# Hybrid DSA/S5 block: x normalised ahead of the gain, single feature tiles handed to the first product, one shared angle table

## The reference, cut to what matters

```python
h    = rms_norm(x, g_norm)              # x (512, 2048), g_norm (2048,)
proj = h @ w_in                         # q, k, v, att_gate, q_idx, k_idx, w_idx, u, ssm_gate, merge
q, k, q_idx, k_idx = partial_rotary(...)       # cos/sin of positions * inv_freq, on the first quarter of each head
att  = dsa_attention(q, k, v, q_idx, k_idx, w_idx)     # indexer scores, top 128 keys, softmax
y_a  = (att * silu(att_gate)) @ w_att_out
s    = gelu(s5_ssm(u, a_re, a_im, log_dt, b, c, d))    # dt = exp(log_dt), per group of 16 channels
s    = s * sigmoid(s @ w_glu + b_glu)
y_b  = (s * silu(ssm_gate)) @ w_ssm_out
gates = sigmoid(merge + b_merge)
out  = rms_norm(x + (gates[0] * y_a + gates[1] * y_b) @ w_out, g_final)
```

## Time and profile before

| | |
|---|---|
| median of 3 runs | 1247.41 us (1247.03 to 1248.04) |
| the profiled execution's own time | 1248.48 us |
| its span, first to last instruction | 1246.7 us |
| PE busy | 1194.5 us, 96% |
| DVE busy | 742.8 us, 60% |
| ACT busy | 415.7 us, 33% |
| POOL busy | 40.4 us, 3% |
| mean granted clock of TensorE | 0.986 of full |

### The profile page before, as it was taken

How to read it: one execution, slowest core, us unless ns; L and a number is a source line. 1 busy time by engine, 2 the same in 40 slices (tenths; PEclk the granted TensorE clock), 3 DMA queues, 4 the chain that set the end, 5 groups by cost and what they waited for, 6 DMA issues and landing times.

```text
span 1246.7 us, 13230 instructions
## 1 busy us (share of the span) xinstructions
PE 1194.5 (96%) x5356; PEld 965.2 (77%) x5356; DVE 742.8 (60%) x1265; ACT 415.7 (33%) x557; POOL 40.4 (3%) x26
## 2 busy tenths in 40 slices
PE   3989799999999999999999999999999999999996
PEld 3789688888787788887666666788888888887885
DVE  5977448999836543258999999744233333513224
ACT  5422233332345442233324342342322222413113
POOL 2000000000000000000101010000000000000002
PEclk8989899999999999999999999999999999999998
DMA  8235332323322124232322222233333333346223
GB/s 267 68 94 113 66 102 68 102 68 102 101 68 68 35 70 115 86 96 77 85 75 68 68 68 68 68 101 102 101 101 94 85 91 101 101 136 236 85 85 135
DMA packets 178637, 119.12 MB, mean 96 GB/s; under 512 B 21777, under 2 KB 169489, under 8 KB 177297
## 3 DMA queue, kind: packets, MB, share of 16 engines
q1 hardware_dynamic: 165920, 117.41, 32.8%
q10 hardware_dynamic: 12656, 0.88, 0.7%
HBM read 114.08 MB, written 4.19 MB: 95 GB/s over the span
## 4 chain that ended last, share of the span: by engine, by line
PE 83%; DVE 12%; ACT 2%; DMA 1%; ACTq 1%; issue 1%; POOLq 0%; SPq 0%; DVEq 0%
PE bank L395 20%; PE bank L396 20%; PE bank L397 20%; PE bank L628 4%; PE bank L630 4%; PE bank L629 4%; DVE w_lo L930 2%; DVE score L1055 2%; DVE small L1054 2%; PE bank L527 1%; PE bank L508 1%; PE bank L565 1%; PE bank L566 1%; DVE score L1043 1%; PE bank L580 1%
## 5 line engine op out<-in xcount | busy, mean ns | idle before, releaser
L395 PE MATMUL bank<-act_hi,w_hi 128*128 128x512 f32 (+1 forms) x1088 | 426.8, 392 | 7.5 <-DVE w_lo L930 7.5
L396 PE MATMUL bank<-act_lo,w_hi 128*128 128x512 f32 (+1 forms) x1088 | 419.3, 385 | 0.0
L397 PE MATMUL bank<-act_hi,w_lo 128*128 128x512 f32 (+1 forms) x1088 | 419.1, 385 | 0.0
L930 DVE TENSOR_TENSOR w_lo<-w_raw,w_hi 128x2048 fp32r<-128x2048 f32 (+1 forms) x98 | 223.5, 2281 | 195.9 <-ACT w_hi L653 194.9
L395 PEld LDWEIGHTS bank<-act_hi,w_hi 128*128 128x128 f32 x1088 | 205.9, 189 | 62.9 <-issue 19.2
L397 PEld LDWEIGHTS bank<-act_hi,w_lo 128*128 128x128 f32 x1088 | 205.8, 189 | 39.1
L396 PEld LDWEIGHTS bank<-act_lo,w_hi 128*128 128x128 f32 x1088 | 206.1, 189 | 34.3
L653 ACT ACTIVATE w_hi<-w_raw 128x2048 fp32r<-128x2048 f32 (+1 forms) x98 | 186.4, 1902 | 106.6 <-DMA w_raw<-in_w_out 105.7
L820 ACT ACTIVATE e_prod<-e_tab,rot 128x64 f32<-128x64 f32 (+1 forms) x64 | 31.8, 496 | 148.6 <-DVE e_tab L1233 90.8
L628 PE MATMUL bank<-w_hi,act_hi 128*128 128x512 f32 x192 | 74.7, 389 | 0.0
L629 PE MATMUL bank<-w_lo,act_hi 128*128 128x512 f32 x192 | 74.7, 389 | 0.0
(11 more groups left out here) (230 smaller groups left out, 1386.7 us busy)
## 6 DMA issues: line engine op xcount, KB each, us to landing
w_raw<-in_w_in SPq DMA_DIRECT2D x68, 1024.0 KB, 5.6
w_raw<-in_w_out SPq DMA_DIRECT2D x16, 1024.0 KB, 5.5
w_raw<-in_w_att_out SPq DMA_DIRECT2D x8, 1024.0 KB, 5.5
xt<-in_x SPq DMA_DIRECT2D x4, 1024.0 KB, 10.0
w_raw<-in_w_ssm_out SPq DMA_DIRECT2D x4, 1024.0 KB, 5.1
res<-in_x SPq DMA_DIRECT2D x4, 1024.0 KB, 11.5
out_dram<-res SPq DMA_DIRECT2D x4, 672.0 KB, 3.1
out_dram<-res SPq DMA_DIRECT2D x4, 352.0 KB, 3.4
```

Source lines behind the costliest of these rows:

```text
L395: nc.tensor.matmul(out_ap, wh, x_hi[k], start=(j == 0), stop=False)
L396: nc.tensor.matmul(out_ap, wh, x_lo[k], start=False, stop=False)
L397: last = nc.tensor.matmul(out_ap, wl, x_hi[k], start=False, stop=(j == n - 1))
L930: v.tensor_tensor(w_lo[:, u % SLOTS, 0:n_el], w_raw[:, u % SLOTS, 0:n_el], w_hi[:, u % SLOTS, 0:n_el].bitcast(F32), ALU.subtract).then_inc ...
```

## The change

- The gain leaves the token-major form. `g_row`, `xg` and POOL's two multiplications go. DVE multiplies x by 1/rms alone (one `tensor_scalar` per token tile); the gain of a feature tile is a column (`small[:, G_COL + k]`) and is applied when the turned tile leaves its bank: as the scale of ACT's copy and in DVE's `scalar_tensor_tensor`.
- The hand-over is by feature tile. PE turns feature tiles 0 to 5 of each token tile as it comes (six banks, each with the four token tiles side by side), then, inside the kidx product, four squares of tile k+6 and two matmuls of tile k. The 16 matmuls with the low part of the weights stand at the end.
- POOL takes `w_lo` of unit 0 and both `w_hi` and `w_lo` of unit 1 (semaphores `early_high`, `early_split`; `wait_split` on PE). POOL first fills the rotary tables with ones and zeros.
- The angles are computed once: rows 0 to 15 and 64 to 79 hold the indexer's frequencies, rows 32 to 63 the heads'. Six Sin activations on 32 rows each follow. The angles now stand behind all of `act_lo` and before `w_lo` of unit 2, and `w_lo` of unit 3 stands directly behind the rotation of the indexer key.
- The small parameters are loaded as rows at the very start, by seven transfers from ACT's queue ahead of its first activation. PE turns the 104 rows in one transpose; DVE copies the columns out. The nine element-wise transfers (six on ACT, three on SP) go.

```diff
@@ sync
             sp.dma_start(ident[:, :], c_ident).then_inc(ident_loaded, 16)
-            sp.dma_start(g_row[:, :], g_norm.to_broadcast([P, D])).then_inc(g_loaded, 16)
...
-                sp.dma_start(g_cols[:, 0:32], b_merge[0].rearrange("(c p) -> p c", p=P)).then_inc(ssm_loaded, 16)
-                sp.dma_start(g_cols[:, 32:36], b_glu[0].rearrange("(c p) -> p c", p=P)).then_inc(ssm_loaded, 16)
-                sp.dma_start(g_cols[:, 36:40], d_skip[0].rearrange("(q g) c -> (g c) q", q=QUADS)).then_inc(ssm_loaded, 16)
@@ gpsimd
-            pool.wait_ge(g_loaded, 16)
-            for i, t in enumerate((1, 2)):
-                pool.wait_ge(x_loaded[t], 16)
-                pool.tensor_tensor(xg[:, i, :], xt[:, t, :], g_row[:, :], ALU.mult).then_inc(xg_ready, 1)
+            for table in (rot_idx, rot_head):
+                pool.memset(table[:, 0, :], 1.0).then_inc(table_set, 1)
+                pool.memset(table[:, 1, :], 0.0).then_inc(table_set, 1)
+            pool.wait_ge(rows_loaded, 7 * 16)
...
+            pool.wait_ge(h_ready, TOK)
+            pool.wait_ge(high_done, 1)
+            pool.tensor_tensor(w_lo[:, 0, 0:n_el], w_raw[:, 0, 0:n_el], w_hi[:, 0, 0:n_el].bitcast(F32), ALU.subtract
+                               ).then_inc(early_split, 1)
+            pool.wait_ge(raw_loaded[1], 16)
+            pool.wait_ge(early_split, 1)
+            pool.tensor_scalar(w_hi[:, 1, :], w_raw[:, 1, :], 1.0, 1.0, ALU.mult, ALU.mult).then_inc(early_high, 1)
+            pool.wait_ge(early_high, 1)
+            pool.tensor_tensor(w_lo[:, 1, :], w_raw[:, 1, :], w_hi[:, 1, :].bitcast(F32), ALU.subtract).then_inc(early_split, 1)
@@ tensor
+            for t in range(TOK):
+                if t == TOK - 2:
+                    pe.wait_ge(rows_ready, 1)
+                    pe.wait_ge(rows_loaded, 7 * 16)
+                    nc.tensor.transpose(banks[7][:, 0:N_ROWS], row_tile[0:N_ROWS, :], ident[0:N_ROWS, 0:N_ROWS]).then_inc(rows_turned, 1)
+                pe.wait_ge(h_ready, t + 1)
+                for k in range(6):
+                    last = turn_x(t, k)
+                    if t == TOK - 1:
+                        last.then_inc(h_turned, 1)
...
+            for k in range(KD):
+                pe.wait_ge(h_low, k + 1)
+                if k + 6 < KD:
+                    for t in range(TOK):
+                        last = turn_x(t, k + 6)
+                    last.then_inc(h_turned, 1)
+                wh = w_hi[:, 0, k * width:(k + 1) * width]
+                nc.tensor.matmul(kidx_out, wh, h_hi[k], start=(k == 0), stop=False)
+                nc.tensor.matmul(kidx_out, wh, h_lo[k], start=False, stop=False)
+            wait_split(0)
+            for k in range(KD):
+                last = nc.tensor.matmul(kidx_out, w_lo[:, 0, k * width:(k + 1) * width], h_hi[k], start=False, stop=(k == KD - 1))
@@ scalar
+            for at_row, src in ((0, a_re ...), (PAIRS, a_im ...), (48, g_norm ...), (64, b_merge ...), (96, b_glu ...), (100, d_skip ...)):
+                act.dma_start(row_tile[at_row:at_row + src.shape[0], :], src).then_inc(rows_loaded, 16)
+            act.dma_start(small[32:32 + PAIRS, LDT_COL:LDT_COL + 2], log_dt[0].rearrange("(j g) -> j g", g=2)).then_inc(rows_loaded, 16)
...
+            for t in range(TOK):
+                rms_of(t)
+            high_through(0)
+            act.wait_ge(cols_ready, 1)
+            for k in range(KD):
+                act.wait_ge(h_turned, k + 1)
+                nc.scalar.activation(act_hi[:, k, :], banks[1 + k % 6][:, :], ACT.Copy, scale=small[:, G_COL + k:G_COL + k + 1]
+                                     ).then_inc(h_high, 1)
+            high_through(2)
...
+            act.wait_ge(ang_ready, 1)
+            for table, first, to, n_ in ((rot_idx, 0, 0, 32), (rot_idx, IDX_DIM, IDX_DIM, 32), (rot_head, 32, 0, 32)):
+                here, there = slice(first, first + n_), slice(to, to + n_)
+                nc.scalar.activation(table[there, 1, :], ang[here, 0, :], ACT.Sin, scale=cols[here, 1:2]).then_inc(table_done, 1)
+                nc.scalar.activation(table[there, 0, :], ang[here, 1, :], ACT.Sin, scale=-1.0, bias=small[here, 237:238]
+                                     ).then_inc(table_done, 1)
+            high_through(3)
+            act.wait_ge(table_done, 6)
             copy_tile(1, q_raw[:, 0, 0:SEQ - P], stream_bank[1][:, 0:SEQ - P])
...
-                    act.dma_start(par[rows, 0, :], a_re[0].rearrange("(j g) p -> g p j", g=2)[g]).then_inc(par_loaded, 16)
-                    act.dma_start(par[rows, 1, :], a_im[0].rearrange("(j g) p -> g p j", g=2)[g]).then_inc(par_loaded, 16)
-                    act.dma_start(par[rows, 2, :], log_dt.rearrange("o (j g) -> g o j", g=2)[g].to_broadcast([STATE, PAIRS])
@@ vector
+            for t in range(TOK):
+                if t == TOK - 1:
+                    dve.wait_ge(rows_turned, 1)
+                    v.tensor_copy(small[:, G_COL:G_COL + KD], banks[7][:, 48:64]).then_inc(cols_ready, 1)
...
+                v.tensor_scalar(xt[:, t, :], xt[:, t, :], small[:, 4 + t:5 + t], None, ALU.mult).then_inc(h_ready, 1)
+            for k in range(KD):
+                dve.wait_ge(h_high, k + 1)
+                v.scalar_tensor_tensor(act_lo[:, k, :], banks[1 + k % 6][:, :], small[:, G_COL + k:G_COL + k + 1],
+                                       act_hi[:, k, :].bitcast(F32), ALU.mult, ALU.subtract).then_inc(h_low, 1)
...
+            link(v.tensor_scalar(ang[:, 0, :], pos_f[:, :], cols[:, 0:1], None, ALU.mult))
+            reduce_angle(ang[:, 0, :], tmp[:, :])
+            v.scalar_tensor_tensor(ang[:, 1, :], ang[:, 0, :], -1.0, ang[:, 0, :], ALU.mult, ALU.max).then_inc(ang_ready, 1)
+            low_through(2)
             dve.wait_ge(kidx_raw, 1)
-            dve.wait_ge(table_done, 2)
+            dve.wait_ge(table_done, 6)
             link(rotate(k_raw[0:IDX_DIM, :], rot_idx, idx_partner, IDX_DIM))
+            low_through(3)
```

More of the change, by code:

```diff
@@ L87, in constants @@
     row = np.arange(P)
[L88 to L99, removed]
+    freq = np.zeros((P, 4), np.float32)
+    for dim, first, rows in ((IDX_DIM, 0, row[0:16]), (IDX_DIM, IDX_DIM, row[64:80]), (HD, 32, row[32:64])):
+        half = dim // 8
+        inv = np.exp(np.float32(-np.log(THETA)) * np.arange(half, dtype=np.float32) * np.float32(2.0 / (2 * half)))
+        freq[rows, 0] = inv[(rows - first) % half]
+        freq[rows, 1] = np.where(rows - first < half, -1, 1)
+    freq[:, 2] = row < STATE
+    freq[:, 3] = row >= STATE
     parity = (row[:, None] // GCH) % 2 == (row[None, :] // STATE)
@@ L379, in _ @@
         def _(pe):
[L380 to L388, removed]
             def product(out_ap, terms, x_hi, x_lo, between):
@@ L428, in _ @@
                 pe.wait_ge(h_ready, t + 1)
[L429 to L435, removed]
-                    last.then_inc(h_turned, 1)
-            pe.wait_ge(h_high, 16)
-            pe.wait_ge(h_low, 9)
@@ L686, in _ @@
                                  ACT.Copy).then_inc(tile_free, 1)
[L688 to L694, removed]
+            act.wait_ge(table_set, 4)
+            act.wait_ge(ang_ready, 1)
[6 more added lines that the diff above has]
+            act.wait_ge(table_done, 6)
             copy_tile(1, q_raw[:, 0, 0:SEQ - P], stream_bank[1][:, 0:SEQ - P])
@@ L704, in _ @@
                 high_through(3 + i)
-            with nc.allow_non_contiguous_dma(reason="one column per pair of groups"):
-                for g in range(2):
-                    rows = slice(STATE * g, STATE * g + STATE)
-                    act.dma_start(par[rows, 0, :], a_re[0].rearrange("(j g) p -> g p j", g=2)[g]).then_inc(par_loaded, 16)
-                    act.dma_start(par[rows, 1, :], a_im[0].rearrange("(j g) p -> g p j", g=2)[g]).then_inc(par_loaded, 16)
-                    act.dma_start(par[rows, 2, :], log_dt.rearrange("o (j g) -> g o j", g=2)[g].to_broadcast([STATE, PAIRS])
-                                  ).then_inc(par_loaded, 16)
             n = 0
@@ L957, in _ @@
             v.memset(small[:, 237:238], PI / 2).then_inc(par_go, 1)
-            def low_of_h(t):
-                for kq in range(4):
-                    n = 4 * t + kq
-                    dve.wait_ge(h_high, n + 1)
-                    part = (slice(None), slice(4 * kq, 4 * kq + 4), slice(t * P, (t + 1) * P))
-                    v.tensor_tensor(act_lo[part], banks[n % 8][:, :].rearrange("p (k n) -> p k n", k=4),
-                                    act_hi[part].bitcast(F32), ALU.subtract).then_inc(h_low, 1)
-            def norm(t):
+            for t in range(TOK):
+                if t == TOK - 1:
+                    dve.wait_ge(rows_turned, 1)
+                    v.tensor_copy(small[:, G_COL:G_COL + KD], banks[7][:, 48:64]).then_inc(cols_ready, 1)
                 dve.wait_ge(rms_done, t + 1)
@@ L971, in norm @@
                 dve.wait_ge(rstd_ready, t + 1)
-                if t in (0, 3):
```

(9 more changed lines are left out.)

91 lines of the change are left out of this document (41 added, 50 removed).

## The result

| | before | after |
|---|---|---|
| median | 1247.22 us (1247.01 to 1248.04, 4 runs) | 1221.02 us (1219.88 to 1221.40, 4 runs) |
| ratio of the two | | 0.9787, 95% interval 0.9775 to 0.9800 |
| profiled execution | 1248.48 us, span 1246.7 | 1219.88 us, span 1218.0 |
| PE busy | 1194.5 us (96%) | 1188.4 us (98%) |
| granted clock | 0.986 | 0.997 |

The change makes the kernel 26.2 us faster by the medians, 28.7 by the spans of the two profiled executions. The forecast was 29.6 us and 1217.8, the range 1214.5 to 1226.

A forecast was written before the change was run, and what follows sets the result against it. PE was taken as the bound, busy 1194.5 of 1246.7 us. The sum 8.9 + 10.5 + 10.7 - 0.5 = 29.6 us, off the median 1247.4, gave 1217.8; its own range 1215 to 1221, with rivals 1214.5 to 1226.

The forecast's parts named there:

- Term 1: Gap at the first query tiles, PE waiting for `w_lo` of unit 3: 8.9 us gained, 5.7 wait and 3.2 slower clock.
- term 4: What is late next: `w_lo` of unit 4 has no margin, so 0.5 us of wait (0 to 2).
- T: The end of the kidx product, forecast at 36.2 us; later steps are counted from it.
- Term 2: Six element-wise transfers on ACT's queue: 10.5 us gained, 7.7 wait and 2.8 slower clock; the three on SP worth 0.
- Term 3: The start: the kidx product ends at 36.2 instead of 46.9, a gain of 10.7 us (8 to 12).
- ACT's early transfers: Seven transfers ahead of ACT's first activation: 0.5 us each, 3.5 in all, ACT free just as x lands.
- The slower rival: ACT's seven early issues delay its first sum of squares; 4.7 us each eats the whole gain; 1261 at 6.7; chance 0.03.
- The lock between POOL and DVE: DVE's angle chain begins only when POOL is done with unit 1, adding 0 to 0.5 us.
- the half-earned start: Rival: the start earns half, through late rows, slow clock or hand-over gaps; gain 24, 1223.5 us; chance 0.16.
- the lasting angle wait: Rival: PE still waits for `w_lo` of unit 4 or unit 1; loses up to 8.9, 1226.7 us; chance 0.12.

The follow-up runs named there:

- sin_early: The changed kernel with one Sin activation over a single column ahead of the wait for the angles: 1219.88 us.
- warm: The changed kernel with 31 extra transposes of the identity into bank 0, around the first token tiles, to keep TensorE busy: 1219.17 us.
- gain_load: The changed kernel with the gain's 1 MB load back, unused, between the identity and x tile 1: 1223.84 us.
- split_loop: The changed kernel with PE doing all remaining transposes first, then all 48 matmuls of the first product: 1223.23 us.
- par6: The changed kernel with the six element-wise transfers back on ACT's queue ahead of the first relu: 1230.81 us.

## Why the prediction was right, and where it was off

*Term 1, 8.9 us, and term 4, minus 0.5.* Between ACT's copy of the key (46.90 before, 36.76 after) and its copy of the first k tile, the two traces differ by 98.5 - 80.2 = 18.3 us; terms 1, 2 and 4 together said 18.9. The tile behind the transfers gives 22.46 - 11.89 = 10.6 of it, so the two others made 7.7 against 8.4 forecast. That unit 4 would be late next was right. Its wait was 0.8 us for 0.5, but it costs more than its length: `sin_early`, in which it is gone, is 80.2 - 79.1 = 1.1 us quicker here. With 1.1 in place of 0.5, term 1 gave 8.8 for 8.9. One link was missing. The Sin table load of 1.28 us stands behind the wait for the angles, so the six Sin end at T + 8.5, not at T + 7.4. `sin_early` shows this is the wait's cause: with the load ahead, the wait is gone.

*Term 2, 10.5 us.* 10.6 between the two traces, 10.2 by putting the six back. The three transfers on SP weren't put back by themselves; that they were worth nothing fits, as the two traces agree to 0.3 us outside the places named.

*Term 3, 10.7 us.* The product ends at 36.72 for 36.2 forecast: 10.1 us. By its steps: the last squares start at 13.58 (13.6), h is ready at 17.4 (17.6), PE's loop begins at 19.75 (19.5) and takes 17.0 us (15.4 at full clock and 1.3 for the clock: 16.7). `warm` takes the slow clock out and leaves 15.6. DVE's difference is 0.74 each rather than the 0.62 to 0.7 assumed, still less than PE's 0.90. `gain_load` and `split_loop` divide the term: about 3 us for the arrival, 3.7 for the interleaving. The rest, some 3 us, wasn't tried by itself. The trace of the kernel before shows what can lie in it: DVE's `tensor_scalar` on the second tile took 4.77 us beside POOL and 1.29 alone, with PE's second block, ACT's copies and ACT's last squares (26.7) in line behind it, and DVE's multiplication of the last tile by the gain took 2.35 us, where one of 1.29 stands now. Whether these 3.5 and 1.1 us are what is left wasn't tried.

*ACT's early transfers.* 3.2 us for seven (0.27 to 0.63 each) for 3.5 assumed; ACT was ready 0.3 us before x. The 0.5 was right partly by luck: the `c_nat` transfers that it was taken from the earlier trace rows move runs of 64 elements, 256 bytes, not the 512 that the prediction says. The slower rival needed 4.7 us for each.

*POOL.* It was done at 27.9, 3 us sooner than assumed: its `tensor_scalar` took 1.91 us, not 4.0, and began 1.1 us earlier, at 21.3. The lock between POOL and DVE, by which the skill's rule put up to 0.5 us on the angles, therefore had no occasion; DVE's chain began at 31.5. The 0.62 and 0.75 us differences out of PSUM ran beside POOL's products in both kernels, as the prediction had it.

*The sum.* 29.6 forecast, 28.7 between the two traces: the steps miss 0.9 us in all. 26.2 between the medians: the other 2.5 are in the base. The prediction took the median to be 1.1 below the profiled execution and kept this distance for the changed kernel. But the profiled execution of before is a long one (1.3 above the median of its runs in the result; all its runs go from 1246.13 to 1249.00), and that of the changed kernel a short one, 1.1 below. The step that was off most is thus the last: a sum read from one execution was given a range of plus and minus 3 about a median, with the scatter of two single executions, 1 us each, left out. The measured 1221.02 stands at the very edge of that range of 1215 to 1221. It lies well inside 1214.5 to 1226 only because that one has room for the two nearer rivals, the half-earned start and the lasting angle wait, and neither of them came about. The two gaps' shares of slow clock, 3.2 and 2.8 us, come from one execution as well; `par6` has 10.1 us for the same gap in its trace against 10.6 before, and the mean granted clock of before was 0.985 to 0.991 from run to run, so they vary. How much of the 2.5 us is the clock and how much the landing of x stays open, as only profiled executions have a trace.

## What to carry to other kernels

Price a stall by the distance between equal products, not by the wait alone: here waits of 5.7 and 7.7 us cost 8.9 and 10.5, since TensorE's clock fell behind them. Here transfers issued on a computing engine's queue cost next to nothing within the slack in front of the next instruction that PE needs, and beyond it PE's wait and the slow clock behind that (three: 0.3 us, six: 10.2), so move slow issues to where the slack is, or make them short. When a stall is removed, write down the whole chain that stands behind it, table loads included, and compare it with the next deadline. Two edits for one stall may be worth nothing each without the other (the early `w_lo` with both chains in place), so put them back one by one before you credit either.

## What the runs showed of the hardware

- A table load stands behind the wait of the activation that needs it: 39.88 us, when the angles were ready, although ACT had been idle for 1.92 us. One small activation ahead moves it. The Trainium skill, ScalarE: Activation LUTs, section "What ACT_TABLE_LOAD costs", gives about 1283 ns for the load and about 1380 more for a drain. The trace agrees on the load, 1.28 us, but no drain is to be seen: in `sin_early` the load starts within 0.01 us of the end of the copy ahead of it, and the Sin 0.02 us after the load's end.
- Transposes alone bring TensorE's clock up: in `warm` 14 transposes take 3.25 us, and six at 13.60 take 0.87 (at 10.81 they took 1.54), without a single product before them. So did the last block of the kernel before, 1.97 us for 16 after three blocks of 3.4 to 3.6. The Trainium skill, TensorE: Matmul & The Clock Gate, section "Part 4: PE-mode transpose", says that the full clock doesn't engage for transposes in TensorE's transpose mode; its figures are for bf16. These are fp32, and the trace calls them MATMUL and doesn't name the mode. Here the clock rose, and the measurement decides.
- A wait of 2.5 us was followed by 3.4 us at 1.2 GHz, which began 0.5 us after the work had resumed; one of 0.8 us, and those of 1.2 us between the bursts of `warm`, were not.
- The same program leaves 1.2 GHz at a different moment: in the first product two slow blocks of transposes in one trace, three in another, 0.8 us in all.
- The first x tile (1 MB) lands 4.9 to 6.1 us after its issue in the traces of the changed kernel and its variants, and the whole start shifts with it; traces of one chip differ less than those of different chips.
- POOL's `tensor_scalar` over 128x2048 took 1.91 us, its two-input form 4.60.
- ACT's copy out of PSUM takes 0.69 us with a column as scale; without one it took 0.60 in the kernel before.
